# The second block's tail in a fused two-block kernel: another order of its instructions on all engines and of three weight loads

## The chip, the cores and the metric

The kernel runs on one core of a Trainium2 chip. The metric is the device time of one execution in microseconds (us), as the median of several runs. A core has TensorE (PE, matrix products; the profile shows its weight loads apart, as PEld), VectorE (DVE), ScalarE (ACT), GpSimd (POOL) and SyncE (SP), which here only issues transfers. Each engine works through its own list of instructions in order, and they meet at semaphores. 16 DMA engines move data between the chip's memory (HBM) and the core's (SBUF); matrix products land in PSUM.

## What is computed

The reference runs two blocks on 256 tokens of width 1024, all in float32. The first has two layers (a mixer with a recurrence, attention and retention; cross attention; a gated feed-forward). The second has one layer. Its tail, cut to what matters here:

```python
attn = windowed_gqa(q, k, v, sink)                       # 8 heads of 64, in 4 pairs
u, vg = jnp.split(jax.nn.gelu(zg), 2, axis=-1)
gm = spatial_gating(u, vg, ln_g, ln_b, w_s, b_s)         # u * (W_s LN(vg) + b)
mix = concatenate([rms_norm(attn, g_a), rms_norm(gm, g_g)], -1)
x = x + gate1 * rms_norm(mix @ w_out, norm_post_mix)
h2 = modulate(rms_norm(x, norm_pre_ffn), shift2, scale2)
aff = softmax(h2 @ w_router)                             # 16 experts
gates, idx = top_k(aff.T, 32)                            # each expert takes 32 of 256 tokens
hid = silu(xs @ w_gate) * (xs @ w_up)                    # per expert, 1024 x 2816
out = (hid @ w_down) * gates                             # per expert, 2816 x 1024
```

The experts' weights are 16 x 3 matrices of 1024 x 2816 float32, 11.5 MB each, 554 MB in all. They are read once.

## The kernel before

There is one function per engine (`tensor_program`, `scalar_program`, `vector_program`, `gpsimd_program`, `sync_program`). The order in which its lines are reached is the order of that engine's instructions; nothing is rescheduled. `up(name)` raises a semaphore when an instruction is done and `at(name)` is the value to wait for; `free(use)` is the wait for a PSUM bank's reader.

Dense weights come in units of 1 MB. SP loads one into one of four slots, ACT rounds it into its high part (L1334), DVE subtracts to get the low part (L1918, or in two halves at L1925; the helper `unit()` calls both for the next units), and PE multiplies with both. The last four units of the program, numbers 137 to 140, are those of `w_out_2`: rows 2 and 3 (they take the gate rows), then 0 and 1 (they take the attention). The low part of unit 137 is made by `low_half`, that of unit 138 by the `unit()` that stands after `values(3)` on DVE.

The second block's tail, in `second()` of each engine:

- Attention runs in a chain per head: PE makes scores, DVE masks and reduces them, ACT exponentiates, PE turns the probabilities (L991, `turned(h)`), ACT copies them out (L1768), PE multiplies a pair of heads with the values (`values(c)`, 128x64 products; pair 3 is heads 6 and 7), and DVE scales into `AT` (L2562, `values(c)`, raising `o2_out`).
- The gate rows: ACT and DVE make gelu of `u` (tanh at L1795, `gelu_out` at L1913), PE makes two `sgu` products (128x64), DVE multiplies (`gated(t)`), the result `GM` is squared (ACT L1828, DVE L2653), POOL takes the power for the root (L2802), ACT and DVE scale (`half_scaled`), PE turns the rows (L575, four 128x128 transposes per bank), ACT and DVE copy them out as high and low part (L1379, L1913), and then `out_unit(2)` can start.
- A step of the heads' chain is put between other work by `beside.step()`; an `out_unit` takes a step after each of its two row tiles. `beside.finish(heads)` runs all that is left of the chain.
- `lc` is a product of the router's weights with the shift (eight 128x16 products), the router's constant part, copied to `LC` by DVE. `busy` issues products whose result nobody reads.

SP meanwhile loads the first expert's `w_gate` in four chunks of 2.9 MB into the buffers b0, b2, b1 and b6 (`opening()`, L2950 to L2966), as soon as the tiles that lie there are no longer needed. Each load is ready for a different reason:

- the first half of b2 when the last `w_in_2` product is done,
- b6, which lies over the attention's values and the gate rows' inputs, when `sgu` 1 has been read and the values of heads 6 and 7 are multiplied (`pv` 7),
- b1, when DVE has scaled those (`o2_out` 7),
- the second half of b2, which lies over the slots of units 137 and 138, when both low parts are made (`slots_split`, L2946).

After these come the chunks of the first `w_up` (L3033, L3016), then all the rest in a ring of buffers, each waiting for the chunk whose place it takes (L2977).

Of the kernel before, what the change touches and what calls it, by code (L numbers as in the profile page):

```python
# [64 lines left out]
BIG = 5632  # L65


class Signals:
# [10 lines left out]
    def up(self, family, *key, by=1):  # L79
        n = self.count[family] = self.count.get(family, 0) + by  # L80
        assert ((family, *key) not in self.value) if self.first else self.value[(family, *key)] == (family, n), (family, key)
        self.value[(family, *key)] = (family, n)
        return self.sem(family), by
# [11 lines left out]
    def at(self, *name):  # L95
        family, n = self.value.get(name, (name[0], 1)) if self.first else self.value[name]
        return self.sem(family), n
# [288 lines left out]
def tensor_program(e, C):  # L386
    up, at, same, M = C.sig.up, C.sig.at, C.sig.same, C.M
    PS, HT, MX, MEM, X, S = M.PS, M.HT, M.MX, M.MEM, M.X, M.S
    beside = Beside()
# [7 lines left out]
    def take(name, hold=False):  # L397
        i, k = C.banks.take(name, hold)
        if k > 1:
            e.wait_ge(C.sig.sem(f"bank{i}"), k - 1)  # L400
        return PS[:, 4 + i, :]
# [7 lines left out]
    def free(*use):  # L409
        return C.free(use)  # L410
# [4 lines left out]
    def mm(o, l, r, start, stop):  # L415
        return e.matmul(o, l, r, start=start, stop=stop, skip_group_check=True)  # L416
# [169 lines left out]
    def busy(name, n, by=M.CST[:, 0:256]):  # L586

        use = ("busy", *name)
        ps = take(use)
        for _ in range(n):  # L590
            ins = mm(ps[:, 0:256], M.ID, by, True, True)
        ins.then_inc(*C.freed(*use))
# [357 lines left out]
    def second():  # L950
# [95 lines left out]
            ins.then_inc(*up("full", "sgu", t))  # L1046
            drop(("sgu", t))
        beside.step()
        ps = take(("lc",))
        e.wait_ge(*at("wr"))  # L1050
        e.wait_ge(*at("gs"))
        for k in range(8):
            ins = mm(ps[:, 0:16], M.small["MT"][:, 16 + k:17 + k].broadcast_to([128, 128]), M.WR[:, k, :], k == 0, k == 7)
        ins.then_inc(*up("full", "lc"))
        beside.finish(heads)
        e.wait_ge(*at("scaled_first", ("gm",), 1))
        e.wait_ge(*at("scaled_second", ("gm",), 0))
        for _ in turning(("gm",), [M.GM[:, 0, :], M.GM[:, 1, :]], 4):
            pass
        busy(("gm", 1), 2)  # L1060
        y = ("mix2",)
        e.wait_ge(*free("turn", ("gm",), 0))
        out_unit("w_out_2", 0, 2, y, of=("heads2",), start=True)
        e.wait_ge(*free("turn", ("gm",), 2))
        rows = attended()
        beside.add(rows)
        out_unit("w_out_2", 0, 3, y)
# [29 lines left out]
        ins.then_inc(*up("full", "lgp", t))  # L1097

    turn_x(0)
    busy(("exp", 0), 2)  # L1100
    turn_x(1)
    logit_parts(0)
    logit_parts(1)
# [213 lines left out]
def scalar_program(e, C):  # L1317
# [8 lines left out]
    def par(name, i=0, n=1):  # L1326
        a = PC[name][0] + i
        return M.PT[:, a:a + n]
# [76 lines left out]
    def run_all(job):  # L1405
        for _ in job:
            pass
# [329 lines left out]
    def second():  # L1737
# [78 lines left out]
        turned(5)  # L1816
        gelu_square("u", 1)
        gelu_tanh("u", 0)
        turned(6)
        gelu_tanh("u", 1)  # L1820
        scores(7)

# [3 lines left out]

        e.wait_ge(*free("sgu", 0))
        e.activation(M.XN[:, 0, 0:512], M.GM[:, 0, :], ACT.Square, accum_out=K["ss4"][:, 0:1]).then_inc(*up("gm_sq"))  # L1828
        turned(7)
        half_scaled(("gm",), M.GM, K["rs2"])  # L1830
        run_all(turning(("gm",), MX, 4, 4, par("nog2", 0, 4)))
        unit()
        e.wait_ge(*at("o2_out", 7))
        e.activation(M.XN[:, 0, 0:512], M.AT[:, 0, :], ACT.Square, accum_out=K["ss4"][:, 1:2]).then_inc(*up("at_sq"))
# [55 lines left out]
def vector_program(e, C):  # L1890
# [628 lines left out]
    def second():  # L2519
# [121 lines left out]
        gelu_poly("u", 0)  # L2641
        head_step(7)
        gelu_poly("u", 1)
        values(2)
        gelu_out("u", 0)

        def gated(t):
# [18 lines left out]
        e.wait_ge(*at("gm_sq"))  # L2666
        ts(K["ms"][:, 0:1], K["ss4"][:, 0:1], 1.0 / 512, EPS, ALU.mult, ALU.add).then_inc(*up("ms", ("gm",), 0))
        factors(7)
        e.tensor_copy(M.LC, full("lc")[:, 0:16]).then_inc(*freed("lc"))
        half_scaled(("gm",), M.GM, K["rs2"])  # L2670
        low_half(here, 0)
        low_half(here, 1)
        run_all(turning(("gm",), MX, 4, 4, par("nog2", 0, 4)))
# [22 lines left out]


    mean_square((("exp",),), at("sq", ("exp",), 0, 1), 0, "ms")
    for a in range(2):
        e.tensor_copy(M.HF[:, 4 * a:4 * a + 4, 128:256], full("x_t", 1, a).rearrange("p (k s) -> p k s", k=4)).then_inc(  # L2700
            *freed("x_t", 1, a))
        if a == 0:
            mean_square((("exp",),), at("sq", ("exp",), 1, 1), 1, "ms")
# [190 lines left out]
def sync_program(e, C, out):  # L2894
# [53 lines left out]
    def opening():  # L2948

        nonlocal c  # L2950
        w = D["w_gate_2"][0, 0].rearrange("(p r) d -> p (r d)", p=128)
        early, half = M.PLACE[0][1] - 1024 - M.PLACE[0][0], BIG // 2
        w0 = D["w_down_2"][0, 0].rearrange("(p r) d -> p (r d)", p=128)
        e.dma_start(M.AHEAD[:, :], w0[:, 0:512 * AHEAD]).then_inc(*up("ahead", by=16))
        e.wait_ge(*at("full", "v", 1, 3))
        e.dma_start(M.BIG[0][:, 0:early], w[:, 0:early]).then_inc(*up("b0", "early", by=16))
        e.wait_ge(*at("full", "ug", 1))
        e.dma_start(M.BIG[0][:, early:BIG], w[:, early:BIG]).then_inc(*up("b0", 0, by=16))
        e.dma_start(M.BIG[2][:, 0:half], w[:, BIG:BIG + half]).then_inc(*up("b2", "early", by=16))
        e.wait_ge(*C.free("sgu", 1))  # L2960
        e.wait_ge(*at("pv", "second", 7))
        e.dma_start(M.BIG[6], w[:, 3 * BIG:4 * BIG]).then_inc(*up("b6", 3, by=16))
        e.wait_ge(*at("o2_out", 7))
        e.dma_start(M.BIG[1], w[:, 2 * BIG:3 * BIG]).then_inc(*up("b1", 2, by=16))
        slots_split(*M.PLACE[2])
        e.dma_start(M.BIG[2][:, half:BIG], w[:, BIG + half:2 * BIG]).then_inc(*up("b2", 1, by=16))  # L2966
        for k in range(4):
            user[place(k)] = k
        c = 4
# [168 lines left out]
```

## Time and profile before

| what | us |
|---|---|
| median of 3 runs | 2232.99 (2232.92 to 2234.08) |
| the profiled execution, its own time | 2234.19 |
| its span in the trace | 2230.9 |
| PE busy | 1693.9 (76%) |
| DVE busy | 838.7 (38%) |
| ACT busy | 550.6 (25%) |
| mean clock granted to TensorE | 0.883 of full |

The profiled execution's own time is its span and 3.3 us around it. Positions below are microseconds from the span's start. The first block and the second block's dense part fill about the first 984 us, the experts the rest. Column `PEclk` is the clock granted to TensorE (1.00 is 2.4 GHz, 0.50 is 1.2 GHz), `DMA share` the mean busy share of the 16 DMA engines; it can pass 1 in short stretches, since a packet is counted where it ends.

### The profile page before, as it was taken

The page shows a single profiled execution, that of the slowest core. Times are in us where ns is not written, and L with a number is a line of the kernel's source. Part 1 is how long each engine was busy: PE and PEld are TensorE (multiplying, and loading weights), DVE is VectorE, ACT ScalarE, POOL GpSimd, SP SyncE. Part 2 cuts the span into 40 slices and gives each one's busy share as a digit, 9 for nine tenths or more (in the row PEclk, how much of TensorE's full clock was granted, in tenths as well). Part 3 has the DMA queues.
Part 4 walks back from the last instruction along what each step waited for, and adds up shares of the span by engine and source line. Part 5 has one row for each costly group of instructions (what it writes and reads, how often), then busy time and mean ns, then how long its engine had stood idle before and what let it go on. Part 6 is the DMA issues. An engine that isn't in the chain of part 4 may idle for free.

```text
span 2230.9 us, 27612 instructions
## 1 busy us (share of the span) xinstructions
PE 1693.9 (76%) x11948; PEld 1105.7 (50%) x11948; DVE 838.7 (38%) x1313; ACT 550.6 (25%) x841; POOL 88.2 (4%) x136
## 2 busy tenths in 40 slices
PE   9999999999999999998555556555665555565555
PEld 8899888899888888864111112111111111111211
DVE  5755788867668886741100100100010010010011
ACT  5745544456545444630000000000000000000000
POOL 1200000012100000000000000000000000000000
PEclk9999999999999999999777777877787787787788
DMA  8445567754547675699999999999999999999997
GB/s 275 129 165 194 184 232 253 236 170 145 197 149 245 227 264 162 233 418 434 433 430 434 431 433 430 433 432 433 431 432 432 431 433 431 431 432 432 430 434 312
DMA packets 159831, 739.70 MB, mean 332 GB/s; under 512 B 5424, under 2 KB 131888, under 8 KB 145760
## 3 DMA queue, kind: packets, MB, share of 16 engines
q1 hardware_dynamic: 157360, 731.27, 81.8%
q0 software_dynamic: 2352, 6.69, 0.9%
q8 instruction: 94, 1.54, 0.3%
q14 instruction: 25, 0.20, 0.0%
HBM read 736.88 MB, written 1.05 MB: 331 GB/s over the span
## 4 chain that ended last, share of the span: by engine, by line
PE 50%; DMA 43%; DVE 3%; ACT 2%; issue 1%; POOL 0%; SPq 0%; DVEq 0%; POOLq 0%; ACTq 0%
PE PS L416 49%; DMA WB<-in_w_down 22%; DMA WB<-in_w_gate 20%; DVE WL L1918 1%; ACT WH L1334 1%; DVE X L1913 1%; PE PS L601 0%; DVE S L1913 0%; DMA W<-in_w_in 0%; POOL T L2802 0%; DVE CN L1910 0%; PE PS L575 0%; PE PS L730 0%; DVE S L2027 0%; DVE S L1910 0%
## 5 line engine op out<-in xcount | busy, mean ns | idle before, releaser
L416 PE MATMUL PS<-WB,XS 128*32 128x352 f32 x3984 | 398.2, 564 | 322.4 <-DMA WB<-in_w_up 194.5
L416 PEld LDWEIGHTS PS<-WB,XS 128*32 128x32 f32 x3984 | 140.9, 132 | 581.0 <-issue 217.8
L416 PE MATMUL PS<-HT,WH 128*128 128x256 f32 (+1 forms) x1456 | 382.2, 338 | 4.8 <-ACT HT L1395 2.2
L1918 DVE TENSOR_TENSOR WL<-W,WH 128x2048 fp32r<-128x2048 f32 x133 | 305.6, 2298 | 129.2 <-ACT WH L1334 129.1
L416 PE MATMUL PS<-WB,CN 128*32 128x512 f32 x1320 | 224.3, 805 | 168.5 <-DMA WB<-in_w_down 168.5
L1334 ACT ACTIVATE WH<-W 128x2048 fp32r<-128x2048 f32 x140 | 268.0, 1915 | 242.1 <-PE PS L416 240.1
L1913 DVE SCALAR_TENSOR_TENSOR CN<-CN,PS 128x352 f32<-128x352 f32 (+1 forms) x68 | 35.4, 539 | 692.9 <-PE PS L416 389.4
L416 PE MATMUL PS<-HT,WL 128*128 128x256 f32 x1064 | 293.9, 282 | 0.0
L416 PEld LDWEIGHTS PS<-HT,WH 128*128 128x128 f32 x1456 | 248.2, 190 | 37.5 <-issue 4.6
L416 PEld LDWEIGHTS PS<-WB,CN 128*32 128x32 f32 x1320 | 54.7, 134 | 328.5 <-DMA WB<-in_w_down 185.9
L416 PE MATMUL PS<-WH,MX 128*128 128x512 f32 x672 | 215.9, 394 | 1.0 <-DVE MX L2398 0.9
L416 PEld LDWEIGHTS PS<-HT,WL 128*128 128x128 f32 x1064 | 201.7, 191 | 0.8
L2793 DVE TENSOR_TENSOR CN<-CN,PS 128x512 f32<-128x512 f32 x56 | 38.5, 688 | 369.6 <-PE PS L416 369.6
L416 PEld LDWEIGHTS PS<-WH,MX 128*128 128x128 f32 x672 | 126.2, 188 | 29.1 <-DVE MX L2398 1.3
L416 PE MATMUL PS<-WL,MX 128*128 128x512 f32 x336 | 131.0, 390 | 0.0
L416 PE MATMUL PS<-CN 128*128 128x256 f32 (+3 forms) x322 | 106.4, 460 | 21.2 <-DVE CN L2783 19.4
L1874 ACT ACTIVATE CN<-PS 128x352 f32<-128x352 f32 x30 | 12.3, 461 | 388.2 <-PE PS L416 388.2
L1881 ACT ACTIVATE CN<-PS 128x256 f32<-128x256 f32 x15 | 5.7, 383 | 395.7 <-PE PS L1181 395.7
L416 PE MATMUL PS<-WH,HT 128*128 128x256 f32 (+1 forms) x544 | 103.2, 286 | 0.1
L1883 ACT ACTIVATE CN<-PS 128x512 f32<-128x512 f32 x15 | 9.0, 597 | 380.0 <-PE PS L416 380.0
L416 PEld LDWEIGHTS PS<-CN 128*128 128x128 f32 (+1 forms) x322 | 55.7, 191 | 66.5 <-DVE CN L2783 31.2
L416 PEld LDWEIGHTS PS<-WH,HT 128*128 128x128 f32 x544 | 86.2, 191 | 0.7 <-issue 0.3
(290 smaller groups left out, 1768.0 us busy)
## 6 DMA issues: line engine op xcount, KB each, us to landing
WB<-in_w_up SPq DMA_DIRECT2D x30, 5632.0 KB, 33.4
WB<-in_w_gate SPq DMA_DIRECT2D x29, 5632.0 KB, 32.6
WB<-in_w_down SPq DMA_DIRECT2D x29, 5632.0 KB, 33.1
W<-in_w_in SPq DMA_DIRECT2D x31, 1024.0 KB, 5.4
S<-in_w_ada SPq DMA_DIRECT2D x24, 1024.0 KB, 5.3
W<-in_w_gate SPq DMA_DIRECT2D x22, 1024.0 KB, 7.9
W<-in_w_up SPq DMA_DIRECT2D x22, 1024.0 KB, 10.3
W<-in_w_down SPq DMA_DIRECT2D x22, 1024.0 KB, 9.7
```

What stands on the lines that cost most here:

```text
L416: return e.matmul(o, l, r, start=start, stop=stop, skip_group_check=True)
L1334: e.activation(M.WH[m % 2][:, :], M.SLOT[m % NW], ACT.Copy).then_inc(*up("high", m))
L1874: e.activation(M.HD[ex][:, 352 * hf:352 * hf + 352], PS[:, hf, 0:352], ACT.Tanh, scale=0.5).then_inc(*up("h_tanh", ex, hf))
L1881: e.activation(M.SG[ex], ps[:, 0:256], ACT.Copy).then_inc(*freed("sg", ex))
L1883: e.activation(M.DN[ex][:, 0, :], PS[:, 4, :], ACT.Copy).then_inc(*up("dn0", ex))
L1913: return e.scalar_tensor_tensor(out=o, in0=a, scalar=s, in1=b, op0=o1, op1=o2)
L1918: e.tensor_tensor(M.WL[i][:, :], M.SLOT[m % NW], M.WH[i][:, :].bitcast(F32), ALU.subtract).then_inc(*up("low", m))
L2793: e.tensor_tensor(o, o, ps, ALU.add).then_inc(*done_)
```

## The change

- PE: the rows of the gates are turned before the head chain's last two steps. `turned(7)` follows them, the values of heads 6 and 7 come inside `out_unit(2)`, after its first row tile. The two `busy` products before that unit, and the two behind the first turned tile of `x`, are gone; the eight `lc` products stand in the latter's place.
- ACT: the tanh of the second half of `u`, the last exponentials and the scaling of the gate rows go ahead of `turned(6)`; turning the gate rows goes ahead of `turned(7)`.
- DVE: the values of heads 4 and 5 go behind the scaling of the gate rows. The copy of `lc` goes behind the first mean square of the router's norm.
- SP: the second half of b2 is issued before b6 and b1.

```diff
--- before.py
+++ after.py
@@ -1046,22 +1046,16 @@
             ins.then_inc(*up("full", "sgu", t))
             drop(("sgu", t))
         beside.step()
-        ps = take(("lc",))
-        e.wait_ge(*at("wr"))
-        e.wait_ge(*at("gs"))
-        for k in range(8):
-            ins = mm(ps[:, 0:16], M.small["MT"][:, 16 + k:17 + k].broadcast_to([128, 128]), M.WR[:, k, :], k == 0, k == 7)
-        ins.then_inc(*up("full", "lc"))
-        beside.finish(heads)
         e.wait_ge(*at("scaled_first", ("gm",), 1))
         e.wait_ge(*at("scaled_second", ("gm",), 0))
         for _ in turning(("gm",), [M.GM[:, 0, :], M.GM[:, 1, :]], 4):
             pass
-        busy(("gm", 1), 2)
+        beside.step()
         y = ("mix2",)
         e.wait_ge(*free("turn", ("gm",), 0))
         out_unit("w_out_2", 0, 2, y, of=("heads2",), start=True)
         e.wait_ge(*free("turn", ("gm",), 2))
+        beside.finish(heads)
         rows = attended()
         beside.add(rows)
         out_unit("w_out_2", 0, 3, y)
@@ -1097,7 +1091,12 @@
         ins.then_inc(*up("full", "lgp", t))
 
     turn_x(0)
-    busy(("exp", 0), 2)
+    ps = take(("lc",))
+    e.wait_ge(*at("wr"))
+    e.wait_ge(*at("gs"))
+    for k in range(8):
+        ins = mm(ps[:, 0:16], M.small["MT"][:, 16 + k:17 + k].broadcast_to([128, 128]), M.WR[:, k, :], k == 0, k == 7)
+    ins.then_inc(*up("full", "lc"))
     turn_x(1)
     logit_parts(0)
     logit_parts(1)
@@ -1816,7 +1815,6 @@
         turned(5)
         gelu_square("u", 1)
         gelu_tanh("u", 0)
-        turned(6)
         gelu_tanh("u", 1)
         scores(7)
 
@@ -1826,9 +1824,10 @@
 
         e.wait_ge(*free("sgu", 0))
         e.activation(M.XN[:, 0, 0:512], M.GM[:, 0, :], ACT.Square, accum_out=K["ss4"][:, 0:1]).then_inc(*up("gm_sq"))
+        half_scaled(("gm",), M.GM, K["rs2"])
+        turned(6)
+        run_all(turning(("gm",), MX, 4, 4, par("nog2", 0, 4)))
         turned(7)
-        half_scaled(("gm",), M.GM, K["rs2"])
-        run_all(turning(("gm",), MX, 4, 4, par("nog2", 0, 4)))
         unit()
         e.wait_ge(*at("o2_out", 7))
         e.activation(M.XN[:, 0, 0:512], M.AT[:, 0, :], ACT.Square, accum_out=K["ss4"][:, 1:2]).then_inc(*up("at_sq"))
@@ -2641,7 +2640,6 @@
         gelu_poly("u", 0)
         head_step(7)
         gelu_poly("u", 1)
-        values(2)
         gelu_out("u", 0)
 
         def gated(t):
@@ -2666,8 +2664,8 @@
         e.wait_ge(*at("gm_sq"))
         ts(K["ms"][:, 0:1], K["ss4"][:, 0:1], 1.0 / 512, EPS, ALU.mult, ALU.add).then_inc(*up("ms", ("gm",), 0))
         factors(7)
-        e.tensor_copy(M.LC, full("lc")[:, 0:16]).then_inc(*freed("lc"))
         half_scaled(("gm",), M.GM, K["rs2"])
+        values(2)
         low_half(here, 0)
         low_half(here, 1)
         run_all(turning(("gm",), MX, 4, 4, par("nog2", 0, 4)))
@@ -2696,6 +2694,7 @@
 
 
     mean_square((("exp",),), at("sq", ("exp",), 0, 1), 0, "ms")
+    e.tensor_copy(M.LC, full("lc")[:, 0:16]).then_inc(*freed("lc"))
     for a in range(2):
         e.tensor_copy(M.HF[:, 4 * a:4 * a + 4, 128:256], full("x_t", 1, a).rearrange("p (k s) -> p k s", k=4)).then_inc(
             *freed("x_t", 1, a))
@@ -2957,13 +2956,13 @@
         e.wait_ge(*at("full", "ug", 1))
         e.dma_start(M.BIG[0][:, early:BIG], w[:, early:BIG]).then_inc(*up("b0", 0, by=16))
         e.dma_start(M.BIG[2][:, 0:half], w[:, BIG:BIG + half]).then_inc(*up("b2", "early", by=16))
+        slots_split(*M.PLACE[2])
+        e.dma_start(M.BIG[2][:, half:BIG], w[:, BIG + half:2 * BIG]).then_inc(*up("b2", 1, by=16))
         e.wait_ge(*C.free("sgu", 1))
         e.wait_ge(*at("pv", "second", 7))
         e.dma_start(M.BIG[6], w[:, 3 * BIG:4 * BIG]).then_inc(*up("b6", 3, by=16))
         e.wait_ge(*at("o2_out", 7))
         e.dma_start(M.BIG[1], w[:, 2 * BIG:3 * BIG]).then_inc(*up("b1", 2, by=16))
-        slots_split(*M.PLACE[2])
-        e.dma_start(M.BIG[2][:, half:BIG], w[:, BIG + half:2 * BIG]).then_inc(*up("b2", 1, by=16))
         for k in range(4):
             user[place(k)] = k
         c = 4
```

**The SP queue**, at the first expert's `w_gate` (`AHEAD` is the start of a later matrix, `WB<-in_w_gate` are b0 and b2, `S<-in_w_gate` is b6, `CN<-in_w_gate` is b1). Before:

```order
L2954 DMA AHEAD<-in_w_down 128x3072
L2956 DMA WB<-in_w_gate 128x4608 [waits s_unit]
L2958 DMA WB<-in_w_gate 128x1024 [waits s_unit]
L2959 DMA WB<-in_w_gate 128x2816
L2962 DMA S<-in_w_gate 128x5632 [waits s_pv,s_bank1]
L2964 DMA CN<-in_w_gate 128x5632 [waits s_o2_out]
L2966 DMA WB<-in_w_gate 128x2816 [waits s_low]
L3033 DMA WB<-in_w_up 128x5632 [waits s_unit,s_low] x2
```

and with the change:

```order
L2953 DMA AHEAD<-in_w_down 128x3072
L2955 DMA WB<-in_w_gate 128x4608 [waits s_unit]
L2957 DMA WB<-in_w_gate 128x1024 [waits s_unit]
L2958 DMA WB<-in_w_gate 128x2816
L2960 DMA WB<-in_w_gate 128x2816 [waits s_low]
L2963 DMA S<-in_w_gate 128x5632 [waits s_pv,s_bank1]
L2965 DMA CN<-in_w_gate 128x5632 [waits s_o2_out]
L3032 DMA WB<-in_w_up 128x5632 [waits s_unit,s_low] x2
```

The load that waits for the low parts now stands in front of the two that wait for the heads.

**PE**, from the second `sgu` product to the first rows of `out_unit(2)` (L991 is `turned`, `S,CN 128x64` are `values`, `WR,T` is `lc`, L575 turns the gate rows, `CN 128x256` is `busy`). Before:

```order
L416 MATMUL PS<-S,CN 128x64 [waits s_pt_out,s_o2_out]
L991 MATMUL PS<-CN 128x128 [waits s_exp,s_pt_out]
L416 MATMUL PS<-WR,T 128x16 [waits s_gs,s_wr,s_bank3]
L991 MATMUL PS<-CN 128x128 [waits s_exp,s_pt_out]
L416 MATMUL PS<-S,CN 128x64 [waits s_pt_out,s_o2_out]
L575 MATMUL PS<-CN,S 128x128 [waits s_bank0,s_scaled_second,s_scaled_first]
L575 MATMUL PS<-CN,S 128x128 [waits s_bank1]
L416 MATMUL PS<-CN 128x256 [waits s_bank2]
L416 MATMUL PS<-WH,MX 128x512 [waits s_sc_out,s_low,s_bank0]
```

and with the change:

```order
L416 MATMUL PS<-S,CN 128x64 [waits s_pt_out,s_o2_out]
L991 MATMUL PS<-CN 128x128 [waits s_exp,s_pt_out]
L575 MATMUL PS<-CN,S 128x128 [waits s_bank3,s_scaled_second,s_scaled_first]
L575 MATMUL PS<-CN,S 128x128 [waits s_bank0]
L991 MATMUL PS<-CN 128x128 [waits s_exp,s_pt_out]
L416 MATMUL PS<-WH,MX 128x512 [waits s_sc_out,s_low,s_bank3]
L416 MATMUL PS<-WH,MX 128x512 [waits s_sc_out]
L416 MATMUL PS<-S,CN 128x64 [waits s_pt_out,s_o2_out]
L416 MATMUL PS<-WH,MX 128x512 [waits s_pt_out]
```

Rows without a wait that follow each of these are left out. The values of heads 6 and 7, the second `S,CN 128x64` row, have moved from before the gate rows to the middle of `out_unit(2)`.

**DVE**, from the scaling of the gate rows (`waits s_rstd`) to the low part of unit 138 (L1918, L1917 with the change). Before:

```order
L1910 TENSOR_SCALAR S<-S,T 128x512 [waits s_rstd]
L1925 TENSOR_TENSOR WL<-W,WH 128x1024 [waits s_high] x2
L1913 SCALAR_TENSOR_TENSOR MX<-PS,PT,MX 128x256 [waits s_hi,s_full]
L1913 SCALAR_TENSOR_TENSOR MX<-PS,PT,MX 128x256
L2562 TENSOR_TENSOR S<-PS,T 128x2x2x64 [waits s_rcp2,s_pv]
L1918 TENSOR_TENSOR WL<-W,WH 128x2048 [waits s_high]
```

and with the change:

```order
L1909 TENSOR_SCALAR S<-S,T 128x512 [waits s_rstd]
L2561 TENSOR_TENSOR S<-PS,T 128x2x2x64 [waits s_rcp2,s_pv]
L1924 TENSOR_TENSOR WL<-W,WH 128x1024 [waits s_high] x2
L1912 SCALAR_TENSOR_TENSOR MX<-PS,PT,MX 128x256 [waits s_hi,s_full]
L1912 SCALAR_TENSOR_TENSOR MX<-PS,PT,MX 128x256
L2561 TENSOR_TENSOR S<-PS,T 128x2x2x64 [waits s_rcp2,s_pv]
L1917 TENSOR_TENSOR WL<-W,WH 128x2048 [waits s_high]
```

The values of heads 4 and 5 have come in behind the scaling. In both orders the low part of unit 138 stands directly behind the scaling of heads 6 and 7.

## Rows read from the trace of the kernel before

**Rows 1.** The page, 40 slices of the span: busy tenths of the DMA engines

```profile
DMA  8445567754547675699999999999999999999997
```

**Rows 2.** Windows: us, busy (count) of PE, PEld, DVE, ACT, POOL; PEclk, DMA share, GB/s

```profile
945.00:1045.00 100.00, 96.32 (x737) 58.72 (x735) 39.03 (x83) 23.79 (x47) 4.72 (x10) 1.00 1.01 428
...
1945.00:2145.00 200.00, 111.12 (x853) 34.54 (x856) 17.53 (x24) 3.98 (x9) 2.27 (x6) 0.78 1.00 432
```

**Rows 3.** The chain that ended last, its end: start us, us, what

```profile
2171.79 33.82 DMA WB<-in_w_down
...
2205.66 14.30 PE PS L416 x88
```

**Rows 4.** Windows, as rows 2, around the start of the expert weights

```profile
933.50:941.00 7.50, 5.83 (x32) 5.56 (x32) 5.96 (x13) 3.22 (x11) 1.04 (x2) 0.66 0.01 6
```

**Rows 5.** Timeline of SP: start us, us, engine, line, what it issues

```profile
940.19 0.33 SPq L2962 DMA_DIRECT2D S<-in_w_gate  x1
944.01 0.33 SPq L2964 DMA_DIRECT2D CN<-in_w_gate  x1
946.87 0.33 SPq L2966 DMA_DIRECT2D WB<-in_w_gate  x1
955.17 11.22 SPq L3033 DMA_DIRECT2D WB<-in_w_up  x3
```

**Rows 6.** Waits of SP, 925 to 985: who for whom, us, times, longest

```profile
SPq L2946 <- DVE WL L1918: 2.5, 1, 2.5
```

**Rows 7.** Timeline of PE: start us, us, what [idle before <- releaser]

```profile
926.55 3.68 PE L416 MATMUL PS<-S 128*128 128x64 f32 x32
930.06 1.95 PE L416 MATMUL PS<-S,CN 128*128 128x64 f32 x16
...
932.29 1.86 PE L416 MATMUL PS<-WR,T 128*128 128x16 f32 x16
...
936.45 3.65 PE L416 MATMUL PS<-S,CN 128*128 128x64 f32 x16 [0.90 <-ACT CN L1768]
939.88 1.92 PE L575 MATMUL PS<-CN,S 128*128 128x128 f32 x8
...
942.87 0.59 PE L416 MATMUL PS<-WH,MX 128*128 128x512 f32 x1
...
969.09 1.16 PE L1085 MATMUL PS<-CN,X 128*128 128x128 f32 x8 [0.70 <-DVE X L1913]
```

**Rows 8.** Timeline of DVE, as rows 7

```profile
934.37 1.29 DVE L1913 SCALAR_TENSOR_TENSOR S<-PS,S 128x512 f32<-128x512 f32 x2
935.69 0.69 DVE L2653 CUSTOM_DVE_ANT_0 CN<-S 128x512 f32<-128x512 f32 x1
...
937.80 0.49 DVE L1910 TENSOR_SCALAR S<-S,T 128x512 f32<-128x512 f32 x1 [0.82 <-POOL T L2802]
938.20 2.35 DVE L1925 TENSOR_TENSOR WL<-W,WH 128x1024 fp32r<-128x1024 f32 x2
941.93 1.72 DVE L1913 SCALAR_TENSOR_TENSOR MX<-PS,PT,MX 128x256 fp32r<-128x256 f32 x4 [1.38 <-ACT MX L1379]
943.57 0.41 DVE L2562 TENSOR_TENSOR S<-PS,T 128x256 f32<-128x256 f32 x1
944.50 2.29 DVE L1918 TENSOR_TENSOR WL<-W,WH 128x2048 fp32r<-128x2048 f32 x1 [0.53 <-ACT WH L1334]
```

**Rows 9.** Timeline of ACT, as rows 7

```profile
932.50 0.60 ACT L1768 ACTIVATE CN<-PS 128x512 f32<-128x512 f32 x1 [5.38 <-PE PS L991]
...
942.56 1.91 ACT L1334 ACTIVATE WH<-W 128x2048 fp32r<-128x2048 f32 x1
```

**Rows 10.** Windows, as rows 2, by the clock's two levels

```profile
932.00:936.00 4.00, 2.78 (x25) 2.47 (x23) 3.31 (x6) 3.19 (x10) 0.00 (x0) 1.00 0.36 148
936.00:942.80 6.80, 6.36 (x27) 6.19 (x28) 4.53 (x13) 2.82 (x7) 1.04 (x2) 0.50 0.27 76
```

**Rows 11.** The chain that ended last, inside `w_out_2`: start us, us, what

```profile
952.31 11.02 PE PS L416 x48
```

## The prediction

> **What bounds the kernel now.** I read the page's slices first. From the eighteenth on (about 950 us) the 16 DMA engines are busy for 90% and more of every slice, up to the last [rows 1]. The windows say the same with the other engines beside it: from 945 to 1045 the DMA share is 1.01 at 428 GB/s, later 1.00 at 432, while PE is busy for 111 of 200 us [rows 2]. So 945 us onward is one stream of weights without a gap, and the compute of the experts fits under it. The chain that ended last confirms it at its end: the last weights land at 2205.6, then come 14.3 us of PE and a short tail [rows 3]. The end is therefore the moment at which the stream starts, plus its bytes at 432 GB/s, plus a tail that the change leaves alone. A microsecond earlier or later at the start of the stream is one at the end; a microsecond of PE, DVE or ACT in the dense tail counts only if it moves a load's issue.
>
> Next, when does the stream start? From 933.5 to 941.0 the DMA engines stand still (share 0.01): what was ready has landed, and nothing more has been issued [rows 4]. The gap ends with SP's load of b6, issued at 940.19; b1 follows at 944.01 and the second half of b2 at 946.87, close enough together that no gap shows, and `w_up` from 955.17 [rows 5]. b6 waited for the values of heads 6 and 7: their PE row starts at 936.45 and takes 3.65 us, to 940.1 [rows 7]. The second half of b2 waited 2.5 us for DVE's low part of unit 138 [rows 6], whose row is 944.50 + 2.29 = 946.79 [rows 8]. **What matters is the time at which the first of these three is issued.**
>
> **The change, step by step.** The gate rows do get ahead, and by much. The two `sgu` products are done at about 930.1 (926.55 + 3.68, less the overlap with the next row at 930.06) [rows 7]. Before, DVE was then held by the values of heads 4 and 5, and the second tanh of `u` on ACT stood behind the copy of head 6, which started only at 932.50 after 5.4 us of waiting [rows 9]. Both holds are gone, so DVE's second gate product (half of 1.29 us) can run at 930.2 to 930.9 instead of ending at 935.7. From the square to the start of DVE's scaling it is 937.80 - 935.69 = 2.1 us [rows 8], so scaling runs at 933.0 to 933.5. Then on DVE: 0.4 us until the next instruction (938.20 - 937.80), 0.41 for the values of heads 4 and 5, 2.35 for both low halves of unit 137, which brings us to 936.2. From the start of the copying of the turned gate rows to the first row of `out_unit(2)` it is 942.87 - 941.93 = 0.94 us [rows 7, 8]. `out_unit(2)` starts at about **937.1** instead of 942.87. PE's transposes (1.92 us at the half clock [rows 7]) and ACT's copies lie beside DVE's 2.8 us and cost nothing; uncovered they could cost those 1.9 us.
>
> Now the load. With the change SP stands before the second half of b2 and waits for the low part of unit 138; b6 and b1 are queued behind. DVE makes that low part directly behind the scaling of heads 6 and 7, which needs their values, and PE makes those only after the first row tile of `out_unit(2)`. So:
>
> - `out_unit(2)` starts: 937.1.
> - Its first row tile is 12 products. 48 of them take 11.02 us at the full clock [rows 11], so 12 take 2.76.
> - The values of heads 6 and 7 take 1.95 us at the full clock (the row of heads 4 and 5, 1.85 to the next row) and 3.65 at the half clock [rows 7].
> - DVE's scaling of them 0.41, the low part 2.29, and 0.08 from its end to SP's issue (946.79 to 946.87) [rows 5, 8]. ACT's high part (1.91 us [rows 9]) can start when ACT has turned the gate rows and copied head 7, near 936.5, and is hidden.
>
> At the full clock that is 937.1 + 2.76 + 1.85 + 0.41 + 2.29 + 0.08 = 944.5, or 4.3 us later than 940.19. The clock decides the rest. It was granted in full until 936.0 and at 0.50 until 942.8, after a stretch in which PE was busy for 2.78 of 4 us with narrow products [rows 10]. With the change PE has even less between 932.5 and 937.1: the transposes, the four of head 7, and nothing else, since the `lc` and `busy` products have left. I expect the half clock again. If it lasts through the row tile (12 products, 2.76 x 3.65 / 1.95 = 5.2 us) the issue comes at 946.9, 6.7 us late; if it lasts through the values too, at 948.8, 8.6 us late. I take a half clock that ends inside the row tile, as it ended 6.8 us after it began before: 5.6 us late, between the two nearest cases.
>
> The Trainium skill, page "TensorE: Matmul & The Clock Gate", section "Part 1: The HAM clock gate", says that the throttled clock is the default and activity releases it. The trace agrees (0.50 in rows 10 after a thin stretch), and by that rule the removed `busy` products speak for the later of my ends.
>
> Of this, the stream can win back what it now loses while it is on: 428 instead of 432 GB/s over 100 us is 0.9 us at most; I take 0.3. The three loads then stand in the queue together (7.2 MB), so the DMA engines don't run dry before `w_up`, which can be issued while they land: its first issue is at 955.17 now, and PE's part up to there is not later. Moved at no cost: the eight `lc` products (1.86 us, in the place of `busy` between the two turned tiles of `x`, where PE now idles 0.70 us more before the row at 969.09 [rows 7]; 0.2 us late at most), their copy, the values of heads 4 and 5. Their cover is the stream itself: it would take several microseconds more on PE before a load is late.
>
> **Sum:** 5.6 - 0.3 = +5.3 us. The profiled execution, 2234.19 (span 2230.9 and 3.3 around it), would become 2239.5. It lies 1.2 above the median, so against the median of 2232.99 the forecast is **2238.3 us**, 0.24% slower. About 0.2% (4.5 us) is what a measurement of this kernel can tell from no change, so the forecast lies just outside.
>
> **The rivals.**
>
> *The end follows PE, not the stream (faster).* Unit 3 of `w_out_2` can start when the low part of 138 is made, at 944.5 at the full clock; now it starts behind the 24 products of unit 2, at 942.87 + 24 x 0.23 = 948.4. So PE's work comes up to 3.9 us earlier: 2232.99 - 3.9 = 2229.1. It holds if the DMA engines have gaps of that size after 985 that PE's loads could fill. Against it: share 1.01 and 428 GB/s in the first 100 us [rows 2], so at most 0.9 us. The Trainium skill, page "Perfetto Trace Analysis", section "Optimization Strategies", would have one optimize whatever leaves the matmul engine idle, which is what this rival pays for. Here the trace speaks against it. Chance 0.08.
>
> *The order of the loads does not do what it says (about the same).* If the second half of b2 were released by unit 137's low part alone, it would be issued at 936.3 and carry 1.4 MB (3.3 us of transfer) in the gap, while b6 would come at about 941.8, 1.6 us late: 1.7 us gained, 2231.3. Against it: that load waited for the L1918 row that ends at 946.79, not for the halves that ended at 940.55 [rows 5, 6, 8]. Chance 0.10.
>
> *The clock stays full.* Then +4.3 - 0.3 = 4.0 us, 2237.0, just within 0.2%. For it: the dense row tile comes early. Chance 0.17.
>
> *The clock stays half through the values.* +8.6 - 0.3, 2241.3. Chance 0.15. The forecast itself, with an end of the half clock anywhere in the row tile or right after it, has 0.50.
>
> **How the numbers follow.** The full-clock case and the early part of the forecast's own range lie within 0.2%, the rest of that and the late case above it. Slower by over 0.2%: 0.15 + 0.50, and less 0.04 for the early part, with a little from the full-clock case, 0.64. Within: 0.28. Faster: 0.08. The range should hold 8 in 10: from 2234.5, which takes in the full clock and an error of 2.5 us in DVE's chain, to 2241.5, the latest case.
>
> **What would show each step.** Right: SP's three loads issued one right after another near 945 to 947, the wait in front of them on DVE's L1917 (near 20 us), the DMA engines idle from 933.5 to then, `out_unit(2)` from 937, the stream at 432 GB/s afterwards and everything from 1050 on shifted by 4 to 7 us. Wrong: b6 or b2 issued before 941, or a stream that starts late and yet ends on time, which would mean that it had slack I did not see.

## The result, and the profile after

The changed kernel takes **2237.57 us** (median of 20 runs, 2236.03 to 2239.47). The kernel before, run beside it, takes 2234.24 (20 runs). The ratio is 1.0015 with a 95% interval of 1.0009 to 1.0021: 3.3 us slower, 0.15%. The forecast was 5.3 us slower, with a chance of 0.64 on a loss of more than 0.2%, which did not come. The result lies in the range, 2234.5 to 2241.5.

The profiled execution took 2236.03 us, 1.84 more than the one of before, though its span is 3.3 us longer (2234.2 and 2230.9): the time around the span, 3.3 us in before, is 1.8 here. Single executions of either kernel scatter by as much as the 3.3 us in question, so the size of the loss is read from the medians, and from the trace only where things stand. To set two traces side by side I align them at SP's load of `AHEAD` (L2953), which lies ahead of all that the change touches: 915.76 in before, 915.62 now.

SP's timeline now, with the columns of [rows 5]:

```profile
915.62 0.47 SPq L2953 DMA_DIRECT2D AHEAD<-in_w_down  x1
...
944.46 0.33 SPq L2960 DMA_DIRECT2D WB<-in_w_gate  x1
944.88 0.38 SPq L2963 DMA_DIRECT2D S<-in_w_gate  x1
945.31 0.42 SPq L2965 DMA_DIRECT2D CN<-in_w_gate  x1
951.19 12.72 SPq L3032 DMA_DIRECT2D WB<-in_w_up  x3
982.50 0.33 SPq L3032 DMA_DIRECT2D WB<-in_w_down  x1
```

The three late loads are issued one right after another, the first of them 28.84 us after `AHEAD`, where it had been 940.19 - 915.76 = 24.43. That is **4.4 us late**. The loads of `w_up` (951.19 for 955.17) and the first of `w_down` come *earlier* than before: PE frees their buffers sooner. What held SP stands in the view of its waits, from 925 to 985:

```profile
SPq L2945 <- DVE WL L1917: 18.7, 1, 18.7
```

2.5 us became 18.7 [rows 6]. The gate rows are as early as the change meant them to be. PE's timeline, as [rows 7]:

```profile
929.91 1.95 PE L416 MATMUL PS<-S,CN 128*128 128x64 f32 x16
...
933.56 1.09 PE L575 MATMUL PS<-CN,S 128*128 128x128 f32 x8 [1.25 <-DVE S L1909]
...
936.95 0.50 PE L416 MATMUL PS<-WH,MX 128*128 128x512 f32 x1 [1.85 <-DVE MX L1912]
...
939.80 1.90 PE L416 MATMUL PS<-S,CN 128*128 128x64 f32 x16
```

The first row of `out_unit(2)` starts at 936.95 instead of 942.87, and the values of heads 6 and 7 now stand behind its first row tile. DVE's timeline, as [rows 8]:

```profile
933.02 0.49 DVE L1909 TENSOR_SCALAR S<-S,T 128x512 f32<-128x512 f32 x1 [0.89 <-POOL T L2801]
933.42 0.42 DVE L2561 TENSOR_TENSOR S<-PS,T 128x256 f32<-128x256 f32 x1
933.75 2.35 DVE L1924 TENSOR_TENSOR WL<-W,WH 128x1024 fp32r<-128x1024 f32 x2
936.02 1.65 DVE L1912 SCALAR_TENSOR_TENSOR MX<-PS,PT,MX 128x256 fp32r<-128x256 f32 x4
941.74 0.42 DVE L2561 TENSOR_TENSOR S<-PS,T 128x256 f32<-128x256 f32 x1 [4.07 <-PE PS L416]
942.08 2.28 DVE L1917 TENSOR_TENSOR WL<-W,WH 128x2048 fp32r<-128x2048 f32 x1
```

DVE stands still for 4.07 us in front of the scaling of heads 6 and 7, with the low part of unit 138, which SP waits for, queued behind it. ACT made the high part long before: its row is 936.17 + 1.94.

Windows of after, with the columns of [rows 2]; the first answers to [rows 4], the last two to [rows 2]:

```profile
933.50:941.00 7.50, 5.58 (x36) 4.85 (x36) 4.17 (x8) 4.07 (x7) 0.00 (x0) 1.00 0.02 8
941.00:945.00 4.00, 3.98 (x21) 3.15 (x21) 3.23 (x4) 0.72 (x2) 0.00 (x0) 1.00 0.00 0
945.00:1045.00 100.00, 94.73 (x731) 57.69 (x730) 36.48 (x80) 23.18 (x46) 4.72 (x10) 0.98 1.01 429
985.00:1005.00 20.00, 20.00 (x244) 9.65 (x242) 1.45 (x4) 1.84 (x5) 0.00 (x0) 1.00 1.02 430
1945.00:2145.00 200.00, 111.81 (x874) 35.34 (x868) 17.53 (x24) 3.98 (x9) 2.27 (x6) 0.78 1.00 432
```

The DMA engines now stand still from 933.5 to 944.5, and from there the stream is as dense as it was. In between, though, before had a thin place that is filled now. The kernel before, the 30 us after the start and the same 20 us:

```profile
945.00:975.00 30.00, 27.77 (x161) 22.04 (x160) 19.38 (x39) 16.13 (x33) 3.20 (x6) 1.00 1.01 432
985.00:1005.00 20.00, 20.00 (x244) 10.03 (x240) 1.45 (x4) 1.95 (x5) 0.00 (x0) 1.00 1.00 407
```

407 instead of 430 GB/s over 20 us is 20 x 23 / 430 = 1.1 us, the part that the stream won back: 4.4 - 1.1 = 3.3. The end of the chain that ended last, as [rows 3], confirms it:

```profile
2175.44 33.56 DMA WB<-in_w_down
2209.00 0.04 issue
2209.04 14.30 PE PS L416 x88
```

The last weights land at 2209.00 instead of 2205.6, some 3.5 us later once the traces are aligned, and the same 14.30 us of PE follow.

### The profile page after: what moved, and what is told of

Same layout as the page of the kernel before. It is cut to its first block, busy times and chain, and to the rows that moved or that the text cites. A ratio compares the mean times of both kernels' runs of the same rounds, so it can differ in the third digit from the quotient of the medians.

```text
span 2234.2 us, 27596 instructions
## 1 busy us (share of the span) xinstructions
PE 1690.1 (76%) x11940; PEld 1102.4 (49%) x11940; DVE 838.7 (38%) x1313; ACT 550.5 (25%) x841; POOL 88.2 (4%) x136
## 4 chain that ended last, share of the span: by engine, by line
PE 50%; DMA 43%; DVE 3%; ACT 2%; issue 1%; POOL 0%; SPq 0%; DVEq 0%; POOLq 0%; ACTq 0%
PE PS L416 48%; DMA WB<-in_w_down 23%; DMA WB<-in_w_gate 20%; DVE WL L1917 1%; ACT WH L1333 1%; PE PS L601 0%; DVE X L1912 0%; DVE S L1912 0%; POOL T L2801 0%; DMA W<-in_w_in 0%; DVE CN L1909 0%; PE PS L730 0%; DVE S L1909 0%; PE PS L575 0%; ACT HT L1394 0%
## 5 line engine op out<-in xcount | busy, mean ns | idle before, releaser
L1917 DVE TENSOR_TENSOR WL<-W,WH 128x2048 fp32r<-128x2048 f32 x133 | 305.6, 2298 | 127.1 <-ACT WH L1333 126.9
## 6 DMA issues: line engine op xcount, KB each, us to landing
W<-in_w_up SPq DMA_DIRECT2D x22, 1024.0 KB, 10.2
```

The source lines that it names most:

```text
L1917: e.tensor_tensor(M.WL[i][:, :], M.SLOT[m % NW], M.WH[i][:, :].bitcast(F32), ALU.subtract).then_inc(*up("low", m))
```

## The experiments

Nine kernels ran, each in five rounds beside the kernel before. "Against before" is the difference of the medians of the same rounds (2234.12 for the first four, 2234.86 for the next three, 2234.18 for the last two). "First issue" is the first of the three late loads, counted from `AHEAD` (24.43 in before).

| kernel | median | ratio, 95% | against before | first issue |
|---|---|---|---|---|
| the change | 2237.57 | 1.0015, 1.0009 to 1.0021 | +3.3 | +4.4 |
| e1, old order of loads | 2235.05 | 1.0005, 0.9996 to 1.0014 | +0.9 | +1.8 |
| e2, order of loads alone | 2239.38 | 1.0025, 1.0015 to 1.0035 | +5.3 | +6.7 |
| e3, low part first | 2232.95 | 0.9995, 0.9986 to 1.0004 | -1.2 | +0.5 |
| e4, heads in the gap | 2229.02 | 0.9977, 0.9968 to 0.9986 | -5.1 | -3.5 |
| e5, and b6 in two parts | 2227.93 | 0.9971, 0.9960 to 0.9982 | -6.9 | -9.1 |
| e6, before, b6 in two parts | 2234.59 | 1.0001, 0.9992 to 1.0010 | -0.3 | -4.5 |
| e7, and b1 in two parts | 2228.49 | 0.9973, 0.9961 to 0.9984 | -6.4 | -14.3 |
| e8, router constants alone | 2234.51 | 1.0000, 0.9991 to 1.0008 | +0.3 | 0.0 |
| e9, e4 with them put back | 2230.45 | 0.9982, 0.9973 to 0.9991 | -3.7 | -2.5 |

### The order of the three loads

Undone in the changed kernel:

```diff
-        slots_split(*M.PLACE[2])
-        e.dma_start(M.BIG[2][:, half:BIG], ...)
         e.wait_ge(*C.free("sgu", 1))
         e.wait_ge(*at("pv", "second", 7))
         e.dma_start(M.BIG[6], w[:, 3 * BIG:4 * BIG]).then_inc(*up("b6", 3, by=16))
         e.wait_ge(*at("o2_out", 7))
         e.dma_start(M.BIG[1], w[:, 2 * BIG:3 * BIG]).then_inc(*up("b1", 2, by=16))
+        slots_split(*M.PLACE[2])
+        e.dma_start(M.BIG[2][:, half:BIG], ...)
```

> The changed kernel with the three loads in their old order: b6, b1, second half of b2. Theory S (the end follows the issue of the first of the three loads): PE's values of heads 6 and 7 end at 941.7 as in the changed kernel, so b6 is issued near 941.7, 1.5 us later than before; the stream ends 1.0 to 1.5 us later than before: 2235.2 to 2235.7 against 2234.2. So two thirds of the loss belong to the order of the loads and one third to the values' place. Rival P (the loss comes from the engines' new order, the loads' order is of no account): as the changed kernel, 2237.6.

The reverse edit, made alone in the kernel before:

> The kernel before with only the loads' order changed: second half of b2 first. Theory S: it is issued at 946.9, when the low part of unit 138 is made, 6.7 us later than b6 was; about 1 us is won back in the stream near 985 to 1050, so +5.7 us: 2239.9. Rival P: as before, 2234.2.

SP's timelines of e1, then of e2:

```profile
942.55 0.33 SPq L2961 DMA_DIRECT2D S<-in_w_gate  x1
942.94 0.41 SPq L2963 DMA_DIRECT2D CN<-in_w_gate  x1
945.18 0.33 SPq L2965 DMA_DIRECT2D WB<-in_w_gate  x1
```

```profile
947.39 0.33 SPq L2961 DMA_DIRECT2D WB<-in_w_gate  x1
947.82 0.38 SPq L2964 DMA_DIRECT2D S<-in_w_gate  x1
948.25 0.42 SPq L2966 DMA_DIRECT2D CN<-in_w_gate  x1
```

In e1 the loss falls from 3.3 us to 0.9, whose interval includes none: the order of the loads costs some **2.4 of the 3.3 us** in the changed kernel. The intervals are 2.7 and 4 us wide and overlap a little, so the times alone leave this rough; the first issue in the traces says 4.4 - 1.8 = 2.6. Alone, in the kernel before, it costs 5.3. The second half of b2 is released last of the three in both kernels (e1: b1 at 942.94, b2 at 945.18), so putting it first makes the other two wait for it. The Trainium skill, page "DMA: Bandwidth & Descriptors", section "Anatomy of one DMA — SWDGE (gpsimd) path", says that DMA engines wait for no semaphores and that any such wait is held on the issuing sequencer. The trace agrees for these queues: with the new order, in either kernel, the wait stands on SP, and the three loads leave within 0.9 us when it ends.

PE's changed order saves 5.26 - 3.33 = 1.9 us with the new order of loads and costs 0.9 with the old one, so the two halves of the change don't look like a sum. By the times alone this is not clear of the intervals; the first issues show it, 6.7 - 4.4 = 2.3 us earlier in the one case and 1.8 later in the other. With the new order the first load hangs on unit 138's low part, which the early gate rows bring forward; with the old one it hangs on the values of heads 6 and 7, which the early gate rows push back (their PE row started at 936.45 [rows 7] and starts at 939.80 now).

### The low part ahead of the values, on DVE

```diff
-        values(3)
         unit()
+        values(3)
         e.wait_ge(*at("o2_out", 7))
```

> The changed kernel, DVE's low part of unit 138 made ahead of its scaling of heads 6 and 7. Nothing else moves; out_unit(2) and the values on PE stay. Theory S: ACT's high part is ready at 938.1, the low part at 940.4, so the second half of b2 is issued near 940.5, b6 near 941.8, b1 near 942.2; the stream starts 0.3 us later than before: 2234.2 to 2234.8. Rival P: 2237.6.

The load order is the new one here; only DVE no longer waits for heads 6 and 7 before it makes the low part. DVE's and SP's timelines:

```profile
939.51 2.29 DVE L1917 TENSOR_TENSOR WL<-W,WH 128x2048 fp32r<-128x2048 f32 x1 [0.47 <-ACT WH L1333]
...
943.10 0.42 DVE L2561 TENSOR_TENSOR S<-PS,T 128x256 f32<-128x256 f32 x1 [1.30 <-PE PS L416]
```

```profile
941.90 0.33 SPq L2960 DMA_DIRECT2D WB<-in_w_gate  x1
943.14 0.33 SPq L2963 DMA_DIRECT2D S<-in_w_gate  x1
943.55 0.45 SPq L2965 DMA_DIRECT2D CN<-in_w_gate  x1
```

This trace runs later as a whole (`AHEAD` at 916.99), so 941.90 is 0.5 us behind before. The swap of two calls takes the kernel from +3.3 to -1.2 us, whose interval includes none. This is the direct test of the chain that the prediction named (values, scaling, low part, SP): with one link out, the loss is gone. I had expected 2234.2 to 2234.8; it came out 1.3 us below that.

### The heads in PE's gaps

In the changed kernel PE stands still for 1.25 and 1.85 us ahead of `out_unit(2)`. Here, on top of e1, the turning of head 7 and the values of heads 6 and 7 go into those gaps, and ACT copies the heads first:

```diff
 tensor_program
         beside.step()
+        beside.step()
         e.wait_ge(*at("scaled_first", ("gm",), 1))
         e.wait_ge(*at("scaled_second", ("gm",), 0))
         for _ in turning(("gm",), [M.GM[:, 0, :], M.GM[:, 1, :]], 4):
             pass
-        beside.step()
+        beside.finish(heads)
...
         e.wait_ge(*free("turn", ("gm",), 2))
-        beside.finish(heads)
 scalar_program
-        half_scaled(("gm",), M.GM, K["rs2"])
         turned(6)
-        run_all(turning(("gm",), MX, 4, 4, par("nog2", 0, 4)))
+        half_scaled(("gm",), M.GM, K["rs2"])
         turned(7)
+        run_all(turning(("gm",), MX, 4, 4, par("nog2", 0, 4)))
```

> The changed kernel with the old order of the loads, and with the last heads put into the idle stretches that the trace of the changed kernel shows: on PE turned(7) before the gate rows are turned and the values of heads 6 and 7 before out_unit(2) (PE idle 1.25 us and 1.85 us there), on ACT turned(6) before and turned(7) right after the scaling of the gate rows. Theory S: values of heads 6 and 7 at 934.5 to 936.4, b6 issued near 936.5, 3.7 us earlier than before, out_unit(2) still at 937. The end up to 3.7 us earlier, less what is lost near 985 where the queue is shallow: 2231 to 2233, faster than both kernels. Rival P: the end moves by PE's part, 3 us earlier than before, about 2231 too, but then e1 must be slow and e3 too. If the clock falls to half in the thin stretch, the values take 3.65 us and the gain shrinks by 1.8.

SP's timeline and a window of e4:

```profile
936.96 0.33 SPq L2961 DMA_DIRECT2D S<-in_w_gate  x1
938.45 0.33 SPq L2963 DMA_DIRECT2D CN<-in_w_gate  x1
940.70 0.33 SPq L2965 DMA_DIRECT2D WB<-in_w_gate  x1
```

```profile
936.00:943.00 7.00, 6.50 (x33) 5.38 (x33) 5.80 (x12) 3.55 (x5) 1.05 (x2) 1.00 0.77 293
```

It beats both kernels: 5.1 us less than before and, by the difference of the two columns, 8.4 less than the change. b6 is issued 3.5 us earlier than before, and the gap of the DMA engines is half filled (share 0.77 from 936 to 943). Most of the change's moves stay in it; what is gone is the order of the loads and the place of the last heads. I had expected 2231 to 2233, with something lost near 985; nothing was lost there (433 GB/s from 985 to 1005), and it came out 2 us below.

### Bringing the stream further forward

b6's second part lies where only the `sgu` products' inputs were, so it can be loaded some us ahead of `pv` 7. Onto e4, and for comparison onto the kernel before:

```diff
         e.wait_ge(*C.free("sgu", 1))
+        e.dma_start(M.BIG[6][:, 1792:BIG], ...)
         e.wait_ge(*at("pv", "second", 7))
-        e.dma_start(M.BIG[6], ...)
+        e.dma_start(M.BIG[6][:, 0:1792], ...)
```

> e4_heads_in_the_gap with b6 loaded in two parts: columns 1792 to 5631 (68% of it, 4.5 us of transfer), which lie only over the gate rows' inputs, when sgu 1 has been read (930.9), the rest when the values of heads 6 and 7 are done. Theory S (the stream's start sets the end): the gap from 933.5 to 937.5 closes, 4 us: 2225. Rival F (the next load behind the first w_up, which waits for PE's first expert product, 62 us behind AHEAD's issue in e4, becomes the late one): the queue runs dry there, so only about 2 us or less: 2227 to 2228, and the windows show an idle stretch near 979 to 981.

> The kernel before, with b6 loaded in the same two parts and nothing else. sgu 1 is read at 935.7, so the stream starts 4.5 us earlier than before and PE's part stays. Theory S alone: 2229.7. Rival F: PE's first expert product stays at 983.8, w_up has landed by 983.1, so the queue runs dry there and most of the gain is lost: 2232 to 2233.5.

The last of this line also loads b1's first 2816 columns as soon as the scores of head 7 are out:

```diff
+        e.wait_ge(*at("sc_out", "second", 7))
+        e.dma_start(M.BIG[1][:, 0:2816], ...)
         e.wait_ge(*C.free("sgu", 1))
...
-        e.dma_start(M.BIG[1], ...)
+        e.dma_start(M.BIG[1][:, 2816:BIG], ...)
```

> e5 with b1 in two parts too: its first 2816 columns (half, 3.3 us of transfer) when DVE has masked head 7's scores, near 925.3, so that the DMA engines never stand still before 938. Theory S: another bit earlier, up to 0.5 us, since e5 has hardly a gap left. Rival F: the end is set by the load behind the first expert product, as in e5: no difference from e5 within 0.5 us.

In e6 the first load comes 4.5 us earlier than before, and the end moves by 0.3 us, which can't be told from nothing and is less than rival F gave. Its windows show where the 4.5 us went:

```profile
945.00:975.00 30.00, 28.08 (x161) 22.37 (x159) 18.87 (x39) 15.66 (x32) 3.21 (x6) 1.00 0.94 387
...
954.00:958.00 4.00, 4.00 (x20) 3.28 (x19) 1.95 (x9) 1.98 (x2) 0.00 (x0) 1.00 0.71 242
...
985.00:990.00 5.00, 5.00 (x60) 2.61 (x52) 0.31 (x1) 0.76 (x2) 0.26 (x1) 1.00 0.95 332
```

387 instead of 432 GB/s over 30 us is 30 x 45 / 432 = 3.1 us lost: the loads of `w_gate` have landed before `w_up` can be issued at 955.75, which waits for PE, and the queue runs dry (242 GB/s from 954 to 958). Another 0.9 us goes at the first `w_down` (332 GB/s over 5 us, where before has 408). Here PE's part is the next thing that is late, and no longer only the first issue; F had that right, but looked for all of the loss at the first `w_down`.

e5 gains 6.9 us, e7 6.4; their intervals overlap, so the second split brings nothing that can be told, though it starts the stream 5 us earlier still. The row of e7 from 975 to 980 shows where something is lost:

```profile
975.00:980.00 5.00, 4.53 (x42) 2.92 (x46) 3.93 (x13) 0.38 (x1) 0.59 (x2) 1.00 0.73 310
```

At 310 GB/s (379 in e5) the stream has run thin again, ahead of the first `w_down`, which PE's part lets go at 979.29. But the two traces differ by more than the split. PE runs the same list in both, and in e7 its granted clock fell (0.72 from 962 to 966, where e5 has 1.00). The second turned tile of `x`, in e5, in e7, and in the change, whose clock fell there too:

```profile
963.29 1.16 PE L1079 MATMUL PS<-CN,X 128*128 128x128 f32 x8
963.43 1.80 PE L1079 MATMUL PS<-CN,X 128*128 128x128 f32 x8
966.61 1.83 PE L1079 MATMUL PS<-CN,X 128*128 128x128 f32 x8
```

So the first `w_down` of e7 is issued 63.3 us after `AHEAD`, against 62.2 in e5. What the second split is worth at the same clock no run shows. e5's 6.9 against e4's 5.1 us is not settled either (0.9971 and 0.9977, intervals 0.9960 to 0.9982 and 0.9968 to 0.9986).

### The router's constants

The prediction's clock term leaned on the narrow products around 932. One edit moves the `lc` products and their copy alone, in the kernel before, as the change does, into the place of two `busy` products; the other puts them back in e4.

```diff
 tensor_program, second()
-        ps = take(("lc",))
-        ...
-        ins.then_inc(*up("full", "lc"))
         beside.finish(heads)
...
     turn_x(0)
-    busy(("exp", 0), 2)
+    ps = take(("lc",))
+    ...
+    ins.then_inc(*up("full", "lc"))
     turn_x(1)
```

> The kernel before with one part of the change alone: the eight lc products and their copy moved behind the first turned tile of x, in the place of the two busy products there; every load, head and gate row stays in its old order. Theory C1 (the router's 16-column products are what lets the clock fall at 936): without them the granted clock is 1.00 from 936 to 943, the values of heads 6 and 7 take 1.95 us instead of 3.65, b6 is issued near 938.3 instead of 940.19, the first out_unit(2) row near 940.5 instead of 942.87; the end comes 1 to 2 us earlier, since part of it is lost again while the queue is shallow (985 to 1005). Theory C2 (the fall comes from what stands after them, heads before gate rows, or from the thin stretch 934 to 936 itself): the clock is 0.50 again, b6 within 0.4 us of before, and the end within 0.5 us of before.

> The heads-in-the-gap version (e4, loads in the old order) with the lc products and their copy put back where they stood in the kernel before, in front of the turning of head 7, and busy back between the turned tiles of x. Theory C1: the clock falls to 0.50 from about 936, the values of heads 6 and 7 take some 3.6 us and end near 941 (with 1 us for the products themselves), b6 is issued 3 to 4 us later than in e4 (936.96), and the end rises from e4's -5.1 us against before to between -2.5 and -1. Theory C2: the clock stays 1.00, b6 comes 0.5 to 1.3 us later than in e4, and the end is at -4.6 to -3.8.

PE's timeline of e8 and its window, then the same window of e9:

```profile
934.76 0.63 PE L991 MATMUL PS<-CN 128*128 128x128 f32 x4 [2.46 <-ACT T L1760]
936.28 3.65 PE L416 MATMUL PS<-S,CN 128*128 128x64 f32 x16 [0.90 <-ACT CN L1767]
```

```profile
936.00:943.00 7.00, 6.72 (x29) 6.46 (x30) 4.67 (x12) 3.03 (x7) 1.04 (x2) 0.52 0.33 105
```

```profile
936.00:943.00 7.00, 6.44 (x38) 5.50 (x37) 6.55 (x12) 3.87 (x7) 0.33 (x1) 1.00 0.58 222
```

Theory C1 falls twice for this stretch: without the 16-column products the clock is half all the same (0.52, the values take 3.65 us), and with them it stays full in e9. Moving them alone is worth nothing, because PE only waits longer for ACT in their place (2.46 us instead of 0.77 behind the products). In e9, where PE has no time to spare, their return delays b6 by 1.0 us. The end is 1.4 us later than e4's, but the two intervals overlap, so that this part of the change pays once the gaps are closed is what the first issue suggests, not what the times show.

## Why the prediction was right, and where it was off

**The bound held.** Where the stream begins sets the end. With PE's order left alone, the loads' order moves the first issue by 6.7 us and the time by 5.3 (e2 against before), and by 2.6 and 2.4 (the change against e1). Over the widest span, from e4 to e2, the first issue moves by 6.67 + 3.50 = 10.2 us and the time by 5.3 + 5.1 = 10.4: one for one. It holds while PE's part keeps the loads behind it ready; e6 and e7 show its limit.

**The chain held to 0.2 us.** Forecast and trace: scaling at 933.0 and 933.02, `out_unit(2)` at 937.1 and 936.95, SP's issue 944.5 at the full clock and 944.46. The row tile took 2.85 us for 2.76, the values 1.94 to DVE's start for 1.85. SP waits on L1917, as foretold, 18.7 us for "near 20", and e3 shows that this chain carries the loss.

**The step that failed is "I expect the half clock again".** It was priced at 1.3 us (5.6 instead of 4.3). The window from 936 to 943 was granted 1.00, so the first load is 4.4 us late, as the rival with a full clock had it (+4.3), which got 0.17. The 5.6 did not follow from its own premise either: a half clock from 936 that lasts 6.8 us, as before, ends at 942.8, behind the row tile's 937.1 + 5.2 = 942.3, and gives at least the 6.7 of the later case; to end inside the row tile it had to begin before 935.5. I argued that PE would be even less busy than the 2.78 of 4 us of [rows 10]. That was so, and the clock did not fall:

```profile
932.00:936.00 4.00, 1.84 (x15) 1.36 (x13) 3.11 (x5) 2.95 (x7) 0.98 (x2) 1.00 0.31 130
936.00:943.00 7.00, 6.05 (x35) 5.32 (x36) 2.93 (x7) 2.83 (x4) 0.00 (x0) 1.00 0.01 2
```

The rule of the Trainium skill's page "TensorE: Matmul & The Clock Gate", section "Part 1: The HAM clock gate", that activity releases the throttle, by which the removed `busy` products spoke for the half clock, is not borne out by the trace here: with them gone, and with more idle time, the clock stayed full. It fell later, to a mean of 0.61 from 966 to 970, behind the moved `lc` products. The term "0.2 us late at most" for these was too small on PE: the turned tile behind them took 1.83 us instead of the 1.16 of e3 to e5. No cost of it shows at the end, since the stream ran on meanwhile (430 GB/s from 985 to 1005).

**The term "I take 0.3" was too small.** The stream won back about 1.1 us. I had bounded it by 0.9 from the mean over 100 us (428 instead of 432); the loss of before sits in 20 of them, at 407 GB/s. The issues of loads suggest why. From issue to landing, before and then after:

```profile
WB<-in_w_down SPq DMA_DIRECT2D x1, 1280.0 KB, 6.9
```

```profile
WB<-in_w_down SPq DMA_DIRECT2D x1, 1280.0 KB, 12.4
```

Before, the first `w_down` load was issued only 6.9 us ahead of its landing, with little queued in front of it. Now the stream is late and PE's part early (982.50 for 983.87, aligned 1.2 us), so the queue is deep there. Every version with this depth at 9 us or more ends 0.8 to 1.7 us better than its first issue alone says (e1, e2, e3, e4, e9 and the change), and e8, as shallow as before, does not (0.0 and +0.3). The three with the stream furthest forward, e5 to e7 (7.3, 5.5 and 5.5 us), end 2.2 to 7.9 us worse than theirs says. That the depth is the cause was not tried by itself.

Together: 5.6 - 0.3 was forecast, 4.4 - 1.1 came out. Of the two errors, both toward too large a loss, the clock made 1.2 us and the regained part 0.8. The measured 3.3 lies nearer to the full-clock rival's 4.0 than to the forecast, and the range held it because it had been drawn wide enough for that rival. In absolute time 2238.3 is only 0.7 above 2237.57; that is luck, since before's median of 20 runs is 1.25 above the median of 3 that the forecast started from. Of the signs named, the issue came at 944.46 for "near 945 to 947", and the end shifted by 3.5 us for "4 to 7".

**The rivals.** That the end follows PE falls: PE's part came earlier and the end later. The Trainium skill's page "Perfetto Trace Analysis", section "Optimization Strategies", which would have one keep the matmul engine going, does not lead to the faster kernel in this stretch: PE's part came 1.2 us earlier, and the end 3.3 us later. That the new order of loads would fill the gap falls too: the second half of b2 does wait for unit 138.

## What to carry to other kernels

A queue that issues transfers in order should meet its waits in the order in which they end: a load put in front because it looks ready holds everything behind it, here for 2.4 us of the end in one kernel and 5.3 in the other. Where a stream of weights sets the end, ask first which of an engine's instructions releases its first late load, and give that one the gap; work that gets ahead of it, however useful, is paid for at the end. Then look for the next load that will be late, since an earlier start is worth only as much as the queue behind it can be kept full.

## What the runs showed of the hardware that was not expected

The granted clock between 936 and 943 does not follow how busy PE was just before. Each kernel has one trace. The mean was near half in before (0.51), e2 (0.57) and e8 (0.52), 0.62 in e6, and full in the change, e1, e3, e4, e5, e7 and e9. From 932 to 936 PE was busy for 2.78 us in before and 3.17 in e6, both of which fell, and 1.84 in the change, which did not:

```profile
932.00:936.00 4.00, 3.17 (x28) 2.86 (x27) 2.96 (x5) 2.80 (x8) 0.00 (x0) 1.00 0.44 182
936.00:943.00 7.00, 6.17 (x29) 5.84 (x30) 5.45 (x15) 3.77 (x9) 1.05 (x2) 0.62 0.86 328
```

These two rows are e6's. What the four that fell have in common is PE's old order of heads and gate rows, with the values of heads 6 and 7 right after a wait for ACT, near 936.3 to 937.0; the seven that stayed full turn the gate rows before that. Whether that order is the cause, or only the moment at which PE stood still, no run here tells. The router's narrow products in their old place are not the cause (e8, e9).

Nor does the order of PE's list settle the clock everywhere. The change, e1 and e3 run the same list on PE, and so do e4, e5 and e7. Right behind the moved `lc` products, around the second turned tile of `x`, the clock fell in the change, e1 and e7 (0.61, 0.67 and 0.72 over the 4 us around it) and stayed full in e3, e4, e5 and e8. What decides between the two is open, and a difference of a microsecond on PE between two single traces can be the clock alone.
